# State-space scan: the 32 decay rows spread over partitions by transfers instead of matmuls, finished on GpSimd, and the time steps computed first

## The reference

```python
dt = softplus(dt + dt_bias);  A = -exp(A_log)
cum = cumsum(dt * A, axis=time)                  # one column for each head
seg = cum[t] - cum[s]
decay = exp(where(s <= t, seg, -inf))            # one 128 x 128 triangle for each chunk and head
w = (C[t] . B[s]) * decay * dt[s]
y[t] = sum_s w * x[s]  + the part that comes from the state of the chunk before
```

## Time and profile before

| | before |
|---|---|
| median of 3 runs | 1345.53 us |
| the profiled execution, time | 1345.03 us |
| its span in the trace | 1343.2 us |
| mean granted TensorE clock | 0.99 |
| TensorE busy | 1294.6 us, 96% |
| VectorE busy | 886.7 us, 66% |
| ScalarE busy | 677.9 us, 50% |
| GpSimd busy | 54.6 us, 4% |
| moved by DMA | 222.26 MB, mean 165 GB/s |

### The profile page before, as it was taken

The page is one execution under the profiler, slowest core; times in us unless marked ns, Lnnn a source line. Parts: engine busy times, 40 slices in busy tenths (PEclk is TensorE's granted clock), DMA queues, the critical chain, the costliest instruction groups (busy, mean ns, idle before and its releaser), DMA issues.

```text
span 1343.2 us, 20050 instructions
## 1 busy us (share of the span) xinstructions
PE 1294.6 (96%) x8551; PEld 1178.6 (88%) x8551; DVE 886.7 (66%) x1176; ACT 677.9 (50%) x846; POOL 54.6 (4%) x62
## 2 busy tenths in 40 slices
PE   6999999999999999998999999999999899999997
PEld 6878999988979999988997777899998877899996
DVE  5666767775446444466876777776668846776666
ACT  3654434444435444535665444375554554565552
POOL 4000000100000000010000010100000100000000
PEclk9999999999999999998999999999999999999999
DMA  9644555655525555544552234555554632655551
GB/s 332 204 126 133 181 158 170 226 184 197 164 94 181 187 188 188 184 147 137 166 182 95 94 116 135 172 185 183 185 188 138 207 99 98 207 184 185 183 181 58
DMA packets 155241, 222.26 MB, mean 165 GB/s; under 512 B 4997, under 2 KB 117377, under 8 KB 155024
## 3 DMA queue, kind: packets, MB, share of 16 engines
q1 hardware_dynamic: 151936, 210.38, 48.7%
q0 software_dynamic: 2928, 10.00, 2.1%
q10 hardware_dynamic: 288, 0.59, 0.1%
HBM read 219.91 MB, written 1.05 MB: 164 GB/s over the span
## 4 chain that ended last, share of the span: by engine, by line
PE 87%; DVE 6%; ACT 3%; issue 2%; POOL 1%; DMA 1%; POOLq 0%; DVEq 0%; SPq 0%; ACTq 0%
PE bank L1882 26%; PE bank L1883 26%; PE bank L1884 26%; DVE wlo L1156 1%; POOL rstd L649 1%; DMA raw<-in_w_in 1%; ACT whi L740 1%; PE bank L2352 1%; PE bank L1974 1%; DVE arena L1607 1%; PE bank L2353 1%; PE bank L2162 1%; DVE bn L1275 0%; PE bank L2049 0%; PE bank L2183 0%
## 5 line engine op out<-in xcount | busy, mean ns | idle before, releaser
L1156 DVE TENSOR_TENSOR wlo<-raw,whi 128x2048 fp32r<-128x2048 f32 (+3 forms) x203 | 453.9, 2248 | 123.6 <-ACT whi L740 122.3
L1882 PE MATMUL bank<-h_hi,whi 128*128 128x256 f32 x1536 | 439.8, 286 | 8.3 <-DVE wlo L1156 5.0
L1883 PE MATMUL bank<-h_lo,whi 128*128 128x256 f32 x1536 | 437.4, 285 | 0.0
L1884 PE MATMUL bank<-h_hi,wlo 128*128 128x256 f32 x1536 | 437.4, 285 | 0.0
L740 ACT ACTIVATE whi<-raw 128x2048 fp32r<-128x2048 f32 (+3 forms) x203 | 379.2, 1882 | 38.8 <-DMA raw<-in_w_in 17.0
L1882 PEld LDWEIGHTS bank<-h_hi,whi 128*128 128x128 f32 x1536 | 297.8, 194 | 10.4 <-DVE wlo L1156 8.4
L1883 PEld LDWEIGHTS bank<-h_lo,whi 128*128 128x128 f32 x1536 | 297.8, 194 | 1.2
L1884 PEld LDWEIGHTS bank<-h_hi,wlo 128*128 128x128 f32 x1536 | 297.6, 194 | 0.0
L1882 PE MATMUL bank<-whi,r_hi 128*128 128x512 f32 (+1 forms) x464 | 180.1, 388 | 2.5 <-DVE r_lo L1180 1.2
L1883 PE MATMUL bank<-wlo,r_hi 128*128 128x512 f32 (+1 forms) x464 | 178.3, 384 | 0.0
L1884 PE MATMUL bank<-whi,r_lo 128*128 128x512 f32 (+1 forms) x464 | 178.0, 384 | 0.0
(11 more groups left out here) (295 smaller groups left out, 1365.4 us busy)
## 6 DMA issues: line engine op xcount, KB each, us to landing
raw<-in_ffn_up SPq DMA_DIRECT2D x44, 1024.0 KB, 5.1
raw<-in_w_in SPq DMA_DIRECT2D x32, 1024.0 KB, 5.9
raw<-in_ssd_in_proj SPq DMA_DIRECT2D x24, 1024.0 KB, 5.4
raw<-in_ffn_down SPq DMA_DIRECT2D x22, 1024.0 KB, 4.9
raw<-in_w_up SPq DMA_DIRECT2D x16, 1024.0 KB, 5.4
raw<-in_w_down SPq DMA_DIRECT2D x16, 1024.0 KB, 4.9
raw<-in_w_xkv SPq DMA_DIRECT2D x8, 1024.0 KB, 5.3
raw<-in_ssd_out_proj SPq DMA_DIRECT2D x8, 1024.0 KB, 5.0
```

Of the source, the lines that this page charges most:

```text
L1156: V.tensor_tensor(wlo[s][:, 0:kt * n], raw[s][:, 0:kt * n], whi[s][:, 0:kt * n].bitcast(F32), ALU.subtract).then_inc(lo_split, 1)
L1882: M(o, a_hi, b_hi, start=start, stop=False)
L1883: M(o, a_hi, b_lo, start=False, stop=False)
L1884: return M(o, a_lo, b_hi, start=False, stop=stop_)
```

## The change

The matmuls that made the decay rows are gone, with their constants. The cumulative sums now lie as 32 rows of 384 values in `crow` (32 partitions); for each head SP issues a transfer that reads one partition's row and writes it into all 128 partitions of a `dec` buffer. GpSimd then adds the head's own sum and clamps at zero (two instructions) and adds the mask (one). ScalarE takes one exponential over 384 columns in place, and VectorE multiplies as before. The transfer of head h waits until `y` of head h-4 is computed; those of heads 1 to 3 wait for the last transposition of x. The four `dec` buffers are one tensor of its own and three rooms of the arena. The inverse square roots of the scan's norms stand between the heads on GpSimd.

Apart from this, the time steps are computed before the loop over `m`: the bias add and one `lo()` on VectorE, softplus, a table load and one `hi()` on ScalarE. The loop makes one call of each less at its end. TensorE transposes the second half of `bc` 0 and 1 right after unit `dt`.

```diff
-        crow = sb("crow", [P, TRI])
-        crow2 = sb("crow2", [2 * SSD_HEADS, TRI], F32R)
+        crow = sb("crow", [SSD_HEADS, TRI])
+        dec0 = sb("dec0", [P, TRI])
...
+            def decay_row(h):
+                if h == 0:
+                    sp.wait_ge(cum_row, 1)
+                elif h < 4:
+                    wait_bank(sp, ("xsN", 7))
+                else:
+                    sp.wait_ge(ssd_y, h - 3)
+                sp.dma_start(dec[h % 4], crow[h:h + 1, :].unsqueeze(1).to_broadcast([1, P, TRI])).then_inc(row_landed[h % 4], 16)
+
+            rows_at = {at[("zz", 0, 0)] + SLOTS - 1: [0], at[("zz", 0, 1)] + SLOTS: [1, 2, 3]}
+            for n, (what, h) in enumerate(SSD_STEPS):
+                if what == "head" and 2 <= h < SSD_HEADS - 2:
+                    rows_at.setdefault(at[("zz", 0, 0)] + SLOTS + n // SSD_PER_UNIT, []).append(h + 2)
             for u, (src, kt, n) in enumerate(units):
+                for h in rows_at.get(u, ()):
+                    decay_row(h)
...
-            for _ in range(4):
-                rsqrt(4)
+            for h in range(SSD_HEADS):
+                pool.wait_ge(row_landed[h % 4], 16 * (h // 4 + 1))
+                d = dec[h % 4]
+                nc.gpsimd.tensor_scalar(d[:, 0:T], d[:, 0:T], negcum[:, 0, 0, h:h + 1], 0.0, ALU.add, ALU.min)
+                nc.gpsimd.tensor_scalar(d[:, T:TRI], d[:, T:TRI], negcum[:, 1, 0, h:h + 1], 0.0, ALU.add, ALU.min).then_inc(pool_step, 1)
+                pool.wait_ge(pool_step, h + 2)
+                diagonal = d.rearrange("p (a t) -> p a t", a=3)[:, 0:3:2, :]
+                nc.gpsimd.tensor_tensor(diagonal, diagonal, big2, ALU.add).then_inc(row_less, 1)
+                if h > 8 and h % 8 == 3:
+                    rsqrt(4)
+            rsqrt(4)
...
+            wait_drained(act, "dt")
+            chain(A(dtv[:, :, :], dtb[:, :, :], ACT.Abs))
+            chain(A(dtv[:, :, :], dtv[:, :, :], ACT.Exp, scale=-1.0))
+            A(dtv[:, :, :], dtv[:, :, :], ACT.Ln, bias=1.0).then_inc(dt_log, 1)
+            act.wait_ge(small_in, 96)
+            A(expa[:, :], row_alog[:, :], ACT.Exp).then_inc(dt_log, 1)
+            nc.scalar.preload_act_table_set("silu_and_others")
+            hi()
...
             for m in range(16):
-                if m >= 2:
+                if 2 <= m < 15:
                     hi()
...
-                        b = wait_bank(act, ("row", h))
-                        if h >= 4:
-                            act.wait_ge(ssd_y, h - 3)
-                        A(dec[h % 4][:, 0:T], b[:, 0:T], ACT.Exp, bias=negcum[:, 0, 0, h:h + 1])
-                        A(dec[h % 4][:, T:TRI], b[:, T:TRI], ACT.Exp, bias=negcum[:, 1, 0, h:h + 1])\
-                            .then_inc(drained[use[("row", h)][0]], 1)
+                        act.wait_ge(row_less, h + 1)
+                        A(dec[h % 4], dec[h % 4], ACT.Exp).then_inc(s_exp, 1)
...
-                        wait_drained(dve, ("row", h))
+                        dve.wait_ge(s_exp, h + 1)
                         b = wait_bank(dve, ("CB", h // 4))
                         V.tensor_tensor(dec[h % 4], dec[h % 4], b[:, 0:TRI], ALU.mult)\
...
-            def ssd_row(h):
-                b = claim(("row", h))
-                diagonal = b[:, 0:2 * T].rearrange("p (a t) -> p a t", a=2)[:, :, 0:P]
-                M(b[:, 0:TRI], pick[:, h:h + 1].to_broadcast([2 * SSD_HEADS, P]), crow2[:, :], start=True, stop=False)
-                M(diagonal, identr[:, :], bigr[:, :].unsqueeze(1).to_broadcast([P, 2, P]), start=False, stop=True)\
-                    .then_inc(fill(("row", h)), 1)
+            def ssd_scores(h):
```

More of the change, by code:

```diff
@@ L109, in constants @@
     c[:, C_IDENT:C_TRI] = np.eye(P)
[L110 removed]
+    c[:, C_TRI:C_BIG] = i[:, None] <= i[None, :]
     hide = np.where(i[None, :] <= i[:, None], 0.0, -3e38)
[L112 to L113 removed]
+    c[:, C_BIG:C_MASK] = np.where(i[:, None] <= i[None, :], 0.0, BIG)
+    c[:, C_MASK:C_INVF] = np.concatenate([hide, np.zeros((P, P)), hide], 1)
     c[:, C_INVF:] = np.float32(1) / np.float32(10000.0) ** (np.arange(0, ROPE, 2, dtype=np.float32) / np.float32(ROPE))
@@ L540, in build @@
         yN = [room(12288 + 1024 * b, NT, MIX) for b in range(2)]
-        dec = [room(14336 + TRI * b, TRI) for b in range(3)] + [crow[:, :]]
+        dec = [dec0[:, :]] + [room(14336 + TRI * b, TRI) for b in range(3)]
         knT, vmN, qnT = room(0, 8, T), room(2048, NT, D), room(4096, 8, T)
@@ L572, in build @@
         normed = sem("normed")
-        cst_r, pick_ready = sem("cst_r"), sem("pick_ready")
+        row_landed = [sem(f"row_landed{i}") for i in range(4)]
+        row_less, s_exp = sem("row_less"), sem("s_exp")
         sb_ln, sb_l_ready, sb_exp, sb_a_ready, sb_av = (sem(n) for n in ("sb_ln", "sb_l_ready", "sb_exp", "sb_a_ready", "sb_av"))
@@ L957, in _ @@
                 A(spad[m % 2][:, :, 3:3 + T], pair(b), ACT.Copy).then_inc(drained[use[key][0]], 1)
[L958 to L968, removed]
                 if m >= 10:
@@ L1573, in _ @@
                 mark(V.memset(spad[b][:, :, 0:3], 0.0))
-            H = SSD_HEADS
-            dve.wait_ge(ident_in, 16)
-            V.tensor_tensor(pick[:, :], ident[0:2 * H, 0:H], ident[0:2 * H, H:2 * H], ALU.add).then_inc(pick_ready, 1)
             dve.wait_ge(dve_step, steps[0])
+            b = wait_bank(dve, "dt")
+            V.tensor_tensor(dtb[:, :, :], b[:, 0:2 * SSD_HEADS].rearrange("p (t h) -> p t h", t=NT),
+                            row_dt[:, :].unsqueeze(1).to_broadcast([P, NT, SSD_HEADS]), ALU.add).then_inc(done("dt"), 1)
+            lo()
             for m in range(16):
-                if m >= 2:
+                if 2 <= m < 15:
                     lo()
@@ L1592, in _ @@
                     b = wait_bank(dve, "cumT")
-                    H2 = 2 * SSD_HEADS
-                    mark(V.tensor_scalar(crow[0:H2, 0:P], b[0:H2, 0:P], -1.0, None, ALU.mult))
-                    V.tensor_scalar(crow[0:H2, 2 * P:TRI], b[0:H2, P:2 * P], -1.0, None, ALU.mult).then_inc(done("cumT"), 1)
+                    H = SSD_HEADS
+                    mark(V.tensor_scalar(crow[:, 0:P], b[0:H, 0:P], -1.0, None, ALU.mult))
+                    V.tensor_scalar(crow[:, 2 * P:TRI], b[0:H, P:2 * P], -1.0, None, ALU.mult).then_inc(done("cumT"), 1)
                     dve.wait_ge(dve_step, steps[0])
                     wait_drained(dve, "cumT")
-                    V.tensor_scalar(crow[0:H2, P:2 * P], crow[0:H2, 2 * P:TRI], crow[0:H2, P - 1:P], None, ALU.add).then_inc(cum_row, 1)
-                if m == 8:
-                    dve.wait_ge(cum_row, 1)
-                    low = slice(SSD_HEADS, 2 * SSD_HEADS)
-                    part(crow2[low, :], crow[low, :], crow2[low, :]).then_inc(cum_row, 1)
+                    V.tensor_scalar(crow[:, P:2 * P], crow[:, 2 * P:TRI], crow[:, P - 1:P], None, ALU.add).then_inc(cum_row, 1)
                 wait_drained(dve, key)
@@ L2304, in _ @@
                 if j >= 2:
-                    b_unit(at[("bc", j)], h_hi, h_lo, one(("bc", j)), between=second_block if j == 2 else None)
+                    b_unit(at[("bc", j)], h_hi, h_lo, one(("bc", j)))
                 if j == 1:
```

21 lines of the change are left out of this document (5 added, 16 removed).

## The result

The changed kernel takes 1441.36 us (median of 4 runs, 1440.02 to 1443.28), the kernel before in the same session 1344.82 us: a ratio of 1.0718, 95% interval 1.0696 to 1.0739. It is 96.5 us slower. The forecast was 1486 us, +141 us: the direction and the step that causes it are right, the forecast growth is nearly half again as large as the measured one; 1441 lies in the given range (1324 to 1530) and just under the forecast's own (1450 to 1545).

What follows compares the result with a forecast made beforehand. TensorE, busy 96% of the span, was taken to bound the kernel before, the row transfers' queue the scan after. 1345.0 - 7.8 (projection stage) + 148.7 (scan) = 1485.9, 1486 us; range 1324 to 1530, the forecast's own 1450 to 1545.

Steps and rivals of the forecast that it cites:

- Bound by TensorE before, and a row's time deciding: Whole kernel: TensorE busy 96% of the span; in the scan, whether one transfer per head keeps 3.65 us decides.
- Part one: Projection stage: time steps first remove the 4.99 us gap before unit `bc` 4 and the low clock behind it, -7.8 us.
- Rows removed, 23.0 us: Scan: 32 row matmuls at 0.72 us each leave TensorE, but all 23.0 us vanish inside its waiting.
- 2.4 us fixed and 7.5 us a row: Scan's row transfers: 2.4 us fixed, plus 7.5 us a row since one partition's reads get one of 16 shares.
- All in one line, row behind row and weights between them: Scan's DMA queue: 31 rows, 232.5 us, plus ten weight transfers between, 25 us; the scan grows by 148.7 us.
- GpSimd, 1.1 us a head: Scan: GpSimd's three instructions take about 1.1 us a head, priced from VectorE's, and cost nothing under the transfer.
- B: Scan rival: transfers quick, GpSimd the bound at 4.2 us a head, about 1357 us; chance 0.09.
- A: Scan rival: rows move at the common DMA rate, so the kernel gets faster, 1330 us (1320 to 1345); chance 0.27.
- The clock hidden: Scan: a lower granted TensorE clock costs nothing; at half clock a slot's matmuls take some 4 us, under 7.5.

Runs made afterwards that it cites:

- e2: Changed kernel with each row transfer reading 128 partitions of a constant instead of one partition of `crow` (decay values wrong): 1355.26 us.
- e3: Changed kernel with the rows written once to HBM and each row transfer reading from there, nothing left out: 1356.81 us.
- e1: Kernel before with only the time steps and the parts of unit `bc` 4 moved ahead of the first taps; row matmuls kept: 1337.61 us.
- e5: e3 with GpSimd adding only the mask; the head's sum is the bias of ScalarE's exponential, in two pieces: 1336.92 us.
- e10: e5 with seven row buffers instead of four, and rows of heads 1 to 3 sent one unit earlier: 1334.42 us.
- e12: Changed kernel with seven row buffers instead of four, and rows of heads 1 to 3 sent one unit earlier: 1433.31 us.
- e11: Changed kernel with consecutive heads reading `crow` partitions 4 apart instead of neighbouring ones (decay values of other heads): 1397.83 us.
- e7: Changed kernel, rows still from SBUF, with GpSimd adding only the mask and the head's sum as the exponential's bias: 1434.20 us.
- e8: Changed kernel with each row in two transfers of 64 destination partitions, the second reading partition h + 32 (zeros): 1440.88 us.
- e9: Changed kernel with each row in two transfers of 64 destination partitions, the second reading partition h + 64 (zeros): 1379.17 us.

## Why the prediction was right, and where its sizes were off

- **Bound by TensorE before, and a row's time deciding**: right. e2 and e3 show that the source alone takes away 85 of 104 us.
- **Part one, -7.8 us**: -7.1 in the trace, -7.3 by itself (e1). The gap and the slow clock behind it went; the next low part came in time.
- **Rows removed, 23.0 us, worth nothing while the transfer bounds**: right as far as the trace shows, where TensorE is idle for 99 us of the scan. Not foreseen: they are worth next to nothing even without the slow transfer (e5, e10).
- **2.4 us fixed and 7.5 us a row**: nearly right. Alone on their way, rows came 7.2 us apart (e12, 27.3 GB/s), and the quickest took 9.6 us to land there, 7.2 behind the fixed part. The 7.2 us that the prediction worked out from the Trainium skill's figure ("SBUF — State Buffer", "Door 1: The DMA port swizzle") is what these rows show. 31 x (7.5 - 7.2) = 9 us of the miss.
- **All in one line, row behind row and weights between them**: wrong, and the larger part of the miss. The step that failed is "from there the queue is the bound: 31 rows x 7.5 = 232.5 us, and ten weight transfers between them (SP's order), 25 us". Rows 1 to 3 go out at 699.2, and in one line even rows of 7.2 us without any weights would make 699.2 + 2.4 + 31 x 7.2 = 924.8; GpSimd started its last row at 910.7, weights and all. So rows passed beside rows for some 14 us, and the 2.5 + 25 us of weights added next to nothing: 42 us too much. For the weights the timeline above shows it: while slices of 71 to 216 GB/s pass between 731 and 740, GpSimd's starts lie 7.45 us apart (729.67 to 737.12), hardly more than 7.2. For the rows, GpSimd's starts are (910.7 - 708.9) / 30 = 6.7 us apart in the mean, less than one row takes alone. At every fourth head the rows come from the next group of partitions that e11 points to, which would let two pass side by side; that this is where the 14 us come from is argued, not tested. Weights aren't free everywhere: in e12 the row behind two of them came 11.3 us after the one before, 4 us more than 7.2.
- **GpSimd, 1.1 us a head**: 2.57 us, too small by a factor of more than two, because its three instructions were priced by VectorE's. It changed the time by little here (e7, with 1.85 us less of it, is 7 us shorter), but with it fast rows give 1357 us, B's time, and not 1330. A's 1330 was not reached by any kernel here (e10: 1334.4, with less work on GpSimd), and A's gain of 23.0 us from the removed rows was not there in e5.
- **The clock hidden**: right for the scan (0.74 there), but not behind it, where 3.6 us more were lost.

The over-counted terms make 9 + 42 = 51 us; 45 separate forecast and measurement. Against them stand the stretch behind the scan (3.6), GpSimd's longer part behind the last row (0.9) and part one (0.7).

## What to carry to other kernels

Before data is spread by DMA out of SBUF, ask how many partitions the source touches: at one, this kernel got 27 GB/s with all 16 engines at it, and HBM was the faster source for the same bytes (a median of 3.3 us to land, against 9.0 at the least). When work is moved off the bound engine, price it in durations of the engine that gets it, and look at the chains beside it too: 23 us of TensorE's work taken away gave nothing in e5, where TensorE then waited for scaling, low parts and products of VectorE and ran at a lower clock. Which of these chains would have to be shorter was not tested. Add the transfers of one queue only if they share what is slow.

## What the runs showed of the hardware

- All 16 DMA engines can show a busy share of 0.8 to 0.9 while 27 to 29 GB/s pass. The share alone would have read as a full DMA system. SP is held up then too: an issue of 0.46 us in e2 took up to 7.5 us.
- DMA reads of partitions h and h + 32 share a limit, h and h + 64 don't (e8 1440.9 us, e9 1379.2 us), and neighbouring partitions share one where those 4 apart don't (e11 1397.8 us). The limit is 27.3 GB/s (e12).
- Two transfers of one queue can pass side by side at twice that rate if they read partitions 64 apart (51 to 60 GB/s in e9).
- GpSimd, over 128 partitions in fp32: add and minimum with a scalar of each partition, 256 columns 1.14 us, 128 columns 0.71 us; addition of two tensors, 256 columns 0.72 us. Single ones of the same instructions took 2.7 to 3.2 us.
- A unit's weights (1 MB) took a median of 17 to 19 us to land beside the rows, and 5 us in e5. No engine waited for weights in the changed kernel's scan: they are issued five units ahead.
